# ScalarE's table set with both logarithm and exponential, named by the kernel ahead of each wait for a norm's sum

## What is computed

```python
def first_block(x, ...):                 # twice, layers l
    h = rmsnorm(x, norm_mix_g[l])
    qa, ka, va, qd, kd, vd, beta, decay, z, gate = split(h @ w_in[l])
    y_attn = grid_attention(rope(rmsnorm(qa)), rope(rmsnorm(ka)), va) @ w_o_attn[l]
    q, k, v = silu(conv5(qd, kd, vd))    # q and k then l2-normed per head of 64
    o = bidir_gated_deltanet(q, k, v, sigmoid(beta), -exp(a) * softplus(decay + b))
    y_dn = (rmsnorm(o) * silu(z)) @ w_o_dn[l]
    g = sigmoid(gate)
    x = x + (g[0] * y_attn + g[1] * y_dn) @ w_out[l]
    u_gate, u_val = split(conv3(rmsnorm(x, norm_ffn_g[l]) @ w_up[l]))
    x = x + (silu(u_gate) * u_val) @ w_down[l]

def second_block(x, mem, ...):           # twice
    z = rmsnorm(x) @ w_in_2[l]
    # three branches: sparse attention (compressed, selected, window),
    # forgetting attention ("fox"), attention over a memory of 256 rows;
    # all queries and keys are rms-normed per head, every branch is gated by a silu
    x = x + (sum of sigmoid gates * branch @ w_branch) @ w_out_2[l]
```

## Time and profile before

| | before |
|---|---|
| median of 3 runs | 3492.17 us (3489.19 to 3505.84) |
| the profiled execution | 3482.06 us |
| its span, first to last instruction | 3480.0 us |
| TensorE busy | 3309.0 us, 95% |
| VectorE busy | 1885.0 us, 54% |
| ScalarE busy | 1542.2 us, 44% |
| mean granted TensorE clock | 0.986 |
| HBM | 70 GB/s over the span |

### The profile page before, as it was taken

The page is one execution under the profiler, slowest core; times in us unless marked ns, Lnnn a source line. Parts: engine busy times, 40 slices in busy tenths (PEclk is TensorE's granted clock), DMA queues, the critical chain, the costliest instruction groups (busy, mean ns, idle before and its releaser), DMA issues.

```text
span 3480.0 us, 61520 instructions
## 1 busy us (share of the span) xinstructions
PE 3309.0 (95%) x26780; PEld 2615.9 (75%) x26780; DVE 1885.0 (54%) x2834; ACT 1542.2 (44%) x2604; POOL 201.6 (6%) x188
## 2 busy tenths in 40 slices
PE   7899999999998899999999998989999989999999
PEld 5577887878875687877788876767788767676787
DVE  6566656666465565656745664453444644434444
ACT  6544223433246434233423365556533455464432
POOL 0031320000000220410000000000000000000000
PEclk9899999999999999999999999999999999999999
DMA  4001103232231001123233231202122212111222
GB/s 145 31 10 49 42 30 109 93 103 91 97 117 43 20 27 50 33 68 110 87 95 103 82 118 56 88 31 68 55 88 76 96 61 88 43 58 58 78 72 94
DMA packets 75212, 249.15 MB, mean 72 GB/s; under 512 B 9280, under 2 KB 10944, under 8 KB 73920
## 3 DMA queue, kind: packets, MB, share of 16 engines
q1 hardware_dynamic: 74944, 245.22, 21.7%
HBM read 237.88 MB, written 6.29 MB: 70 GB/s over the span
## 4 chain that ended last, share of the span: by engine, by line
PE 81%; DVE 8%; ACT 7%; issue 3%; DMA 0%; SPq 0%; ACTq 0%; DVEq 0%
PE psum L519 78%; PE psum L696 2%; ACT s_tmp L1242 2%; DVE s_tmp L1937 1%; ACT L1242 1%; ACT s_w L1242 1%; DVE s_nm L2016 1%; DVE s_ffy L1937 1%; DVE s_w L1934 1%; DVE s_xb L1934 1%; ACT s_E L1242 0%; DVE s_tmp L1934 0%; DMA s_stage<-w 0%; PE psum L606 0%; DVE psum L1934 0%
## 5 line engine op out<-in xcount | busy, mean ns | idle before, releaser
L519 PE MATMUL psum<-s_h,s_w 128*128 128x512 f32 (+1 forms) x6864 | 1657.8, 398 | 22.6 <-DVE s_h L1934 8.9
L519 PEld LDWEIGHTS psum<-s_h,s_w 128*128 128x128 f32 (+1 forms) x6864 | 1281.9, 189 | 330.7 <-issue 45.9
L1934 DVE TENSOR_TENSOR s_w<-s_stage,s_w 128x1024 fp32r<-128x1024 f32 (+2 forms) x468 | 528.4, 1130 | 404.6 <-ACT s_w L1242 403.1
L1242 ACT ACTIVATE s_w<-s_stage 128x1024 fp32r<-128x1024 f32 (+2 forms) x468 | 451.2, 966 | 279.7 <-PE psum L519 256.3
L519 PE MATMUL psum<-s_ffa,s_w 128*128 128x512 f32 x1056 | 249.0, 396 | 3.8 <-DVE s_ffa L1934 3.8
L519 PEld LDWEIGHTS psum<-s_ffa,s_w 128*128 128x128 f32 x1056 | 197.5, 187 | 54.2 <-DVE s_ffa L1934 6.4
L519 PE MATMUL psum<-s_oR,s_w 128*128 128x512 f32 (+1 forms) x960 | 215.3, 375 | 0.0
L1242 ACT ACT_TABLE_LOAD x160 | 205.3, 1283 | 7.1 <-DVE s_tmp L1937 3.6
L2016 DVE TENSOR_REDUCE s_nm<-psum 128x1 f32<-128x512 f32 (+3 forms) x288 | 138.1, 521 | 122.3 <-PE psum L519 121.8
L1242 ACT ACTIVATE s_E<-psum,s_nm 128x256 f32<-128x256 f32 (+3 forms) x224 | 114.3, 515 | 186.6 <-DVE s_nm L2016 186.5
L1242 ACT ACTIVATE s_tmp<-psum 128x512 f32<-128x512 f32 (+2 forms) x154 | 87.4, 568 | 247.0 <-PE psum L519 243.1
(11 more groups left out here) (284 smaller groups left out, 3471.9 us busy)
## 6 DMA issues: line engine op xcount, KB each, us to landing
s_stage<-w SPq DMA_DIRECT2D x192, 512.0 KB, 3.3
s_stage<-wup SPq DMA_DIRECT2D x88, 512.0 KB, 3.3
s_stage<-wo SPq DMA_DIRECT2D x32, 512.0 KB, 3.3
s_stage<-wdn SPq DMA_DIRECT2D x32, 512.0 KB, 3.6
s_stage<-wdn SPq DMA_DIRECT2D x16, 384.0 KB, 3.1
spill<-s_x SPq DMA_DIRECT2D x2, 2048.0 KB, 8.7
s_stage<-woa SPq DMA_DIRECT2D x16, 256.0 KB, 2.7
s_x<-spill SPq DMA_DIRECT2D x2, 2048.0 KB, 8.0
```

The lines of the kernel that those rows point to most:

```text
L519: return self.e.matmul(out, left, right, start=first, stop=last, skip_group_check=True)
L1242: return self.e.activation(out, src, func, **kw)
L1934: return self.e.tensor_tensor(out, a, b, op)
```

## The change

Nothing is taken from the arithmetic. The dummy logarithms go. A method `logs()` names the set `natural_log_exp_and_others` unless the flag `has_ln` says that it is in; a Tanh clears the flag, and every Ln calls `logs()` first. Besides, `logs()` is called by name ahead of the waits of `norm`, `qk_end` and `memory`, right after the Square in `project_end` (one turn before the wait), at the last step of `streamed` and at the start. `root`, `scalars`, `forgetting` and `outputs` have no call of their own, so there the set is named, if it is missing, by `f` behind the wait.

```diff
--- before.py
+++ after.py
@@ -394,7 +394,7 @@
         self.x, self.h = sb("x", [128, 8, T]), sb("h", [128, 2, 8, T], F32R)
         self.stage = sb("stage", [128, 3, 1024])
         self.half = [[sb(f"w{i}{j}", [128, 1024], F32R) for j in range(2)] for i in range(3)]
-        self.eps, self.one, self.ln = sb("eps", [128, 1]), sb("one", [128, 1]), sb("ln", [128, 1])
+        self.eps, self.one = sb("eps", [128, 1]), sb("one", [128, 1])
         self.valid = sb("valid", [128, 1])
         self.tmp6 = sb("tmp", [128, 6, T])
         self.rope = sb("rope", [128, 2, T])
@@ -1239,6 +1239,10 @@
 
 
     def f(self, out, src, func, **kw):
+        if func == ACT.Ln:
+            self.logs()
+        elif func == ACT.Tanh:
+            self.has_ln = False
         return self.e.activation(out, src, func, **kw)
 
     def halves(self, n):
@@ -1248,9 +1252,11 @@
             self.w.wait_ge(*self.at("prod", n - 3))
         self.f(self.m.half[n % 3][0][:, 0:kt * w], self.m.stage[:, n % 3, 0:kt * w], ACT.Copy).then_inc(*self.up("hi", n))
 
-    def table(self):
-        self.f(self.m.ln[:, :], self.m.one[:, :], ACT.Ln).then_inc(*self.up("act_table", self.tables))
-        self.tables += 1
+    def logs(self):
+
+        if not self.has_ln:
+            self.e.preload_act_table_set("natural_log_exp_and_others")
+            self.has_ln = True
 
     def narrow(self, key, w, made=None):
         self.ahead(key)
@@ -1297,7 +1303,7 @@
         for c in range(8):
             step(c)
             if c == 7:
-                self.table()
+                self.logs()
             next(raw)
         next(raw, None)
 
@@ -1420,10 +1428,10 @@
 
     def run(self):
         m = self.m
-        self.tables = 0
+        self.has_ln = False
         self.slots = [(m.tmp6[:, i, :], ()) for i in range(3)]
+        self.logs()
         self.w.wait_ge(*self.at("vec_set", "one"))
-        self.table()
         self.one_ahead()
         for n, _ in enumerate(self.raw("in")):
             if n in (7, 11):
```

## The result

| | before | after |
|---|---|---|
| median | 3490.68 us (3485.72 to 3505.84, 4 runs) | 3457.23 us (3452.71 to 3459.18, 4 runs) |
| ratio | | 0.9895, 95% interval 0.9863 to 0.9927 |
| the profiled execution, its span | 3482.06, 3480.0 us | 3456.99, 3455.2 us |
| mean granted TensorE clock | 0.986 | 0.985 |

The kernel became 33 us faster between the medians, 1.05% by the ratio. Two executions far outside all others (7121.68 us among the six of e3, 5817.94 among the 29 of the kernel before in the runs that e5 to e8 are set against) are left out of every ratio. The forecast was 19 us less (3473.2); 3457 is at the low end of its range, and faster by over 0.5% had the smaller of the two large chances. The sign was right, the size was not.

A forecast was written before the change was run, and what follows sets the result against it. TensorE, busy 95% of the span, was taken as the bound, leaving at most 171 us open. Terms 3.4 + 3.4 + 4.4 + 6.0 + 0.4 + 1.4 = 19.0 us, off the median 3492.17, gave 3473.2 us, range 3456 to 3487.

The forecast's parts named there:

- No DMA, matmul or VectorE instruction is added: Whole kernel: no such work is added; only what is queued behind a named load, the next high half, gets later.
- The sum of the loads: Whole kernel: all terms, the clock's 6.0 us included, add up to 19.0 us saved.
- Query stage, layer 0: First layer's queries and keys: without the loads the matmul at 76.50 us comes at 73.1, 3.4 us saved.
- Layer 1: Query stage of the second gated layer: TensorE itself ends the wait and VectorE runs without pause, so 0 saved.
- Projection stages: 84 to 165 us, twice: 3.0 us gained less 1.3 for a new load ahead of a Tanh, 1.7 a layer.
- Second projections with their clock: 300 to 350 us, twice: 2.2 us a layer from loads, 3.0 a layer from the clock no longer falling.
- Later layers: Four stretches of the two later layers: 1.4 us saved in all; loads elsewhere there are hidden beside TensorE work.
- What a switch costs: ScalarE's table switch: a load of 1.283 us with 0.02 on either side, 1.4 at most with lost overlap.
- The first (no clock back): Rival: the clock does not come back, only hidden parts shrink; 13.0 us saved, 3479 us; chance 0.22.
- The second (more than forecast, 3463): Rival: clock falls at 76 and 97 us go, projection stage undervalued; 29 us saved, 3463 us; chance 0.12.
- The third: Rival: moved loads become the new path, delaying weights where Tanhs alternate; up to 20.4 us slower, 3513 us; chance 0.08.
- The fourth: Rival: the named sets are passed over and every Exp still loads; 160 loads stay, 3492 us; chance 0.06.

The follow-up runs named there:

- e3: Changed kernel with the combined set named only by f, behind the wait, the early logs() calls removed; ratio 0.9923.
- e5: Kernel before with the combined set only in the query stages of the gated layers, tile ln kept; ratio 0.9973.
- e8: Changed kernel with the next needed set named behind project_end's Tanh and ahead of waits for a projection's product and a key's transpose; ratio 0.9961.
- e9: Changed kernel with the removed 4-byte tile ln left in its place, unused; ratio 0.9944, 3470.98 us.
- e1: The changed kernel run once more, nothing altered, for a closer ratio and a second trace; ratio 0.9908, 3459.06 us.
- e11: Changed kernel with the Tanh set named right behind a projection's scaled copy when a Tanh comes next; ratio 0.9888, 3450.84 us.
- e10: Kernel before, loads and dummies kept, with tile ln allocated behind all others, giving the other tiles the changed kernel's addresses; ratio 0.9984.
- e7: Kernel before with the combined set only in the two later layers, tile ln kept; ratio 1.0002.

## Why the prediction was right in sign and wrong in size

**The step that failed: "No DMA, matmul or VectorE instruction is added".** True, and from it I took the matmuls' durations as fixed. The first line of the diff takes a tile out, which moves all tiles behind it by 32 bytes, and 2688 matmuls of weights (1056 + 768 + 672 + 192) run 5 to 6 ns faster for it. That is 13.5 to 15.5 us of matmul time, 12 us in the median (e9 against e1); it was in no term, no bound and no rival. Without it the median would have been 3471.0 (e9), against a forecast of 3473.2.

**The sum of the loads: right, in part by luck.** 19.0 forecast; 19.5 by the ratio of e9, 17.6 between its medians. But the terms below miss in both directions and cancel, and between the first trace of the kernel before, from whose rows they were taken, and that of e9 there are only 11.2 us (3480.0 to 3468.8). The clock is part of it: the runs of e9 have 0.985 on the mean, those of the kernel before 0.983, by the 2.5 us above some 6 of the 19 (an estimate).

**Query stage, layer 0: 3.4 forecast, 6.4 measured** (76.50 to 70.07), of which 1.6 was there already at 60 us. I let only two of ten earlier loads reach the last key, since I took ScalarE to wait for TensorE before it. In the trace it was ScalarE that had fallen behind, one whole product; without the loads it caught up, and the low half that was to stay in the way left it. **Layer 1: 0, right**: the gap still is 2.08.

**Projection stages: 1.7 a layer forecast, 0.6 and 0.7 measured in the first trace, 1.9 and 0.7 in the second** (between the like matmuls at 76.50 and 166 us, and in the second layer). At 97.24 the gain of the stage was 2.5 to 3.2 us, but from there on 1.0 to 2.6 us were given back, mostly more than the 1.28 that I charged to the Tanh. The load that I named for it is real (146.93): in e11, which moves it, the gap is 1.43 shorter and these stretches gain 3.6 and 4.0 us. That the whole kernel is faster for it is likely and not shown, since the intervals of e11 and e1 overlap.

**Second projections with their clock: 2.2 + 3.0 a layer forecast, 5.2 and 5.2 measured** between the like matmuls at 300 and 362 us and at 1312 and 1372 of the kernel before (first traces; 5.2 in both layers in e1 as well). The 3.0 for the clock stand on like stretches of the kernel before: from 349.21 to the end of the twelve matmuls 7.8 us at a granted clock of 0.56, from 329.85 on 4.7 us at 1.00. The gaps shrank to 1.14, a little more than said, and the twelve matmuls behind them took 3.02 us at full clock in both layers (from 342.45 and from 1335.89). The clock gave back elsewhere, though: 2115 to 2131 us at 0.57, some 6 us, which no term had.

**Later layers: 1.4 forecast, -0.7 with an interval of 3.8 either way**: in agreement, though 56 loads went.

**What a switch costs.** Without a load an Exp starts 0.03 us after its Ln ends (66.37 + 0.69 to 67.09), with one 1.30: the difference is the 1.28 of the load. The forecast counts a load with no more than that; its sum was 19.0 us, and e9 measured 19.5.

**The rivals.** The first (no clock back) fell: the clock came back at 350 us in both traces (1.00 from 300 to 360 us, 0.94 before). The second (more than forecast, 3463) came nearest in time and by the wrong mechanism: the walk had undervalued the query stage, not the projections, and what brought it near 3463 was the tile. The third was refuted in the changed kernel, yet e8 is just that mechanism, loads moved ahead of work that TensorE waits for. The fourth fell: 80 loads.

**Against what.** The term for the clock was made against an execution with few falls: its mean clock was 0.986, that of the 62 runs of the kernel before beside the experiments 0.982. The second trace is 16 us longer. So the medians are 33 us apart and the first two traces only 25.

## What to carry to other kernels

Read a diff's declarations as well as its instructions: here a tile of 4 bytes that went moved every tile behind it by 32, and that was worth 12 us. When a big engine's busy time changes and its work doesn't, compare the mean durations of the same groups in both traces. Count a table load where it stands: ahead of a longer wait its 1.28 us were hidden (142.64 in e11, with a gap of 2.02 us instead of 3.45), ahead of a ready instruction on the path they were paid nearly in full (5.30 instead of 4.09 in e8). And take two traces of the kernel before when the clock moves in it.

## What the runs showed that I had not expected

- The time of an fp32r matmul of 128x512 went with where its moving operand starts in a partition: 390 ns at a multiple of 128 bytes, 392 at 64 past one, 396 at 32 past one (the `s_ffa` group). It is no rule for all shapes: those of 128x256 on `s_oR` take 286 ns at a multiple of 128 bytes and 283 at 32 or 64 past one, and the 64x64 matmuls (`s_xb,s_tmp`, 219 ns) did not change.
- VectorE's 32 products `s_xb<-s_cstm,s_xb` look like a second case of it, 1429 ns on the mean before and 1358 after, and are not one:

```profile
L1944 DVE TENSOR_TENSOR s_xb<-s_cstm,s_xb 128x512 f32<-128x512 f32 x32 | 40.6, 1326 | 0.0
```

  is e9, with the addresses of the kernel before, and

```profile
L1935 DVE TENSOR_TENSOR s_xb<-s_cstm,s_xb 128x512 f32<-128x512 f32 x32 | 43.9, 1428 | 0.0
```

  e10, with those of the changed kernel. The mean hides two kinds: in all fourteen traces such a product takes either under 0.7 us (154 of 448) or 1.7 to 1.8 us (294), and GpSimd is at work during at least two thirds of each long one and at most a sixth of each short one. Before, 22 of 32 are long, after 20, in e9 19. No kernel here moved GpSimd's work to test it.
- Whole executions of the kernel before differ by 16 us of span (3480.0 and 3495.6) with the same instructions and nearly the same gaps, through the granted clock (0.986 and 0.979).
- Fifty-six table loads fewer, 72 us of ScalarE's time, changed the whole by no more than 4 us either way (e7).
